# Fetching the output product's operands beside the last head pair, routing tables by one-hot products, and fillings copied by ScalarE

## The reference, cut to what matters

```python
def hybrid_layer(x, ...):
    proj = x @ w_in                                   # 2816 columns
    pool_out = multiscale_pool(proj[..., :256], pool_w, pool_scale)
    rwkv_out = rwkv7_mix(proj[..., 256:], ...)        # 12 heads of 64
    mixed = concatenate([pool_out, rwkv_out]) @ w_out
    h = layer_norm(ALPHA * x + mixed, ln1_g, ln1_b)
    ffn = hierarchical_moe(h, ...)
    return layer_norm(ALPHA * h + ffn, ln2_g, ln2_b)

def hierarchical_moe(h, ...):                         # top group, two experts of 32
    dest = pstart[e_sorted] + (arange(m) - start[e_sorted])
    row_tok = zeros(m_pad, int32).at[dest].set(tok_sorted)   # table: row -> token
    block_expert = minimum(searchsorted(pend, block_start, side='right'), 31)
    for each block of 128 rows:                       # 47 blocks here
        xb = h[row_tok[block]]
        ys = (silu(xb @ exp_gate[e]) * (xb @ exp_up[e])) @ exp_down[e]
```

## Time and profile before

| what | us |
|---|---|
| median of 3 runs (4409.91 to 4419.05) | 4418.75 |
| the profiled execution's own time | 4415.78 |
| its span, first to last instruction | 4414.0 |
| TensorE busy | 3847.3 (87%) |
| VectorE, ScalarE, GpSimd busy | 1659.9, 1159.3, 560.0 |
| mean granted TensorE clock | 0.948 |

### The profile page before, as it was taken

The page is one execution under the profiler, slowest core; times in us unless marked ns, Lnnn a source line. Parts: engine busy times, 40 slices in busy tenths (PEclk is TensorE's granted clock), DMA queues, the critical chain, the costliest instruction groups (busy, mean ns, idle before and its releaser), DMA issues.

```text
span 4414.0 us, 56437 instructions
## 1 busy us (share of the span) xinstructions
PE 3847.3 (87%) x24468; PEld 2362.1 (54%) x24468; DVE 1659.9 (38%) x2549; ACT 1159.3 (26%) x1953; POOL 560.0 (13%) x523
## 2 busy tenths in 40 slices
PE   7899999879699999378898988988688899989989
PEld 3466656544277776034455555555344466546654
DVE  2455455522211111742344444444121544354431
ACT  1222222210011111022233333333111344434440
POOL 0121212101200000320111110100000200020001
PEclk8999999979899999688999999999798999999999
DMA  3000000022599997750000000000310000000001
GB/s 99 15 16 20 16 16 21 1 107 96 167 387 364 367 368 283 261 164 10 15 15 15 15 15 15 5 6 20 108 39 20 10 1 1 12 1 1 1 29 67
DMA packets 110174, 352.07 MB, mean 80 GB/s; under 512 B 14151, under 2 KB 40118, under 8 KB 91750
## 3 DMA queue, kind: packets, MB, share of 16 engines
q1 hardware_dynamic: 86038, 290.10, 18.1%
q0 software_dynamic: 9584, 33.04, 2.2%
q10 hardware_dynamic: 14304, 25.32, 1.7%
HBM read 301.68 MB, written 46.74 MB: 79 GB/s over the span
## 4 chain that ended last, share of the span: by engine, by line
PE 71%; DVE 12%; issue 6%; DMA 4%; POOL 3%; ACT 3%; SPq 1%; ACTq 0%; POOLq 0%; DVEq 0%
PE ps L2222 9%; PE ps L1509 7%; PE ps L1871 7%; PE ps L383 7%; PE ps L2839 6%; PE ps L2240 4%; PE ps L1898 4%; PE ps L1526 4%; PE ps L1139 2%; PE ps L2547 2%; DVE sb L1845 2%; PE ps L2780 2%; PE ps L2801 1%; PE ps L450 1%; PE ps L461 1%
## 5 line engine op out<-in xcount | busy, mean ns | idle before, releaser
L2222 PE MATMUL ps<-sb 128*128 128x512 f32 x960 | 473.9, 611 | 57.7 <-DVE sb L2353 22.1
L1871 PEld LDWEIGHTS ps<-sb 128*128 128x128 f32 x2624 | 298.0, 144 | 340.3 <-ACT sb L1879 131.4
L1871 PE MATMUL ps<-sb 128*128 128x128 f32 x2624 | 427.5, 287 | 48.0 <-ACT sb L1855 18.5
L1879 ACT ACTIVATE sb<-ps 128x512 f32<-128x512 f32 x400 | 238.8, 597 | 791.8 <-PE ps L1871 791.8
L1855 ACT ACTIVATE sb<-ps,sb 128x1280 f32<-128x1280 f32 (+1 forms) x288 | 352.0, 1229 | 143.3 <-DVE sb L1848 140.5
L383 PE MATMUL ps<-sb 128*128 128x512 f32 x704 | 357.0, 622 | 3.4 <-DMA sb<-in_w_in 3.4
L1509 PE MATMUL ps<-sb 128*128 128x256 f32 x1504 | 342.2, 381 | 2.1 <-DMA sb<-in_exp_down 1.3
L2839 PE MATMUL ps<-sb 96*128 96x512 f32 (+1 forms) x768 | 337.5, 533 | 0.0
L1886 DVE COPY sb<-ps 128x512 f32<-128x512 f32 x256 | 176.9, 691 | 415.4 <-PE ps L1871 415.2
L1898 PEld LDWEIGHTS ps<-sb 128*64 128x64 f32 x5248 | 290.2, 139 | 72.1 <-ACT sb L1879 37.0
L1898 PE MATMUL ps<-sb 128*64 128x128 f32 x5248 | 325.9, 279 | 2.9 <-DVE sb L1886 1.6
(11 more groups left out here) (343 smaller groups left out, 4812.0 us busy)
## 6 DMA issues: line engine op xcount, KB each, us to landing
sb<-in_exp_gate SPq DMA_DIRECT2D x47, 1024.0 KB
sb<-in_exp_up SPq DMA_DIRECT2D x47, 1024.0 KB
sb<-in_exp_down SPq DMA_DIRECT2D x47, 1024.0 KB
sb<-in_l_w_mod ACTq DMA_DIRECT2D x12, 2048.0 KB
d_ys<-sb SPq DMA_DIRECT2D x47, 512.0 KB, 14.1
sb<-d_x SPq DMA_DIRECT2D x40, 512.0 KB
sb<-in_l_w_in SPq DMA_DIRECT2D x3, 4096.0 KB, 13.2
sb<-in_w_in SPq DMA_DIRECT2D x22, 512.0 KB, 4.2
```

The costliest lines, as they stand in the source:

```text
L1871: ins = k.pe.e.transpose(k.bank(6)[:, 128 * j:128 * j + 128], self.Pb[g % 2][:, 1280 * b + 128 * c:1280 * b + 128 * c + 128], k.f(C_ID, 128))
L1879: k.act.e.activation(self.PT[:, xs[0]:xs[-1] + 1, :], k.bank(6)[:, 0:128 * len(xs)].rearrange("p (j t) -> p j t", j=len(xs)), ACT.Copy).th ...
L2222: ins = pe.e.matmul(k.bank(5), lhs[:, kk, :], w[:, kk, 512 * half:512 * half + 512], start=kk == 0, stop=kk == 7)
```

## The change

1. **Output product.** The barrier after `mixers` goes. A new object `Ahead` fetches `w_out` into the place of the (now used up) x and projection weights, six mixed rows, the router rows, then the seventh mixed row, two x tiles and the norm rows, from two steps (`ahead`, 0) and (`ahead`, 1) on SyncE, placed behind the last filling and between the merges of the last pair. The eighth mixed row isn't fetched: the product reads `fsq` in SBUF and waits for it only at k = 7. The order inside a tile becomes half 0, half 1 up to k = 3, transposes of the tile before, half 1 from k = 4, router of the tile before.
2. **Routing.** The 16 scatters, the zeroing, the read-back and the transpose go. VectorE makes two one-hot tables (`block`, times the token number, and `place`), and TensorE multiplies them, 16 matmuls of 128x128 by 128x47. SyncE's weight fetches now wait for `beI` alone. Slices: 0 before the counts, 1 and 2 after them, 3 after the row tables; 4 and 5 are fetched at block 43 of the loop and multiplied behind it, the remaining adds move to tiles 1 to 7 (two in tile 7).
3. **Fillings.** `b'z` goes to banks 6 and 7 in matmuls of its own, and ScalarE copies it into `zb` without a mask; VectorE keeps the wide masked copy. GpSimd's level masks wait for ScalarE's copies. `k_next[:2]` moves from ahead of the filling to the steps beside the merges.
4. **Pooling.** `pool_mm` 0 stands behind project(3), and `pool_mm` 1 behind the k projection of pair 0.

```diff
-    for j in range(2):
-        order += project(2 + j) + [("pool_z", j), ("pool_sum", j), ("pool_mm", j)]
+    order += project(2) + [("pool_z", 0), ("pool_sum", 0)] + project(3) + [("pool_mm", 0), ("pool_z", 1), ("pool_sum", 1)]
-    order += k_next + weave(r_next, decay(0) + [("kk", 0), ("kk_sq", 0)])
+    order += k_next + [("pool_mm", 1)] + weave(r_next, decay(0) + [("kk", 0), ("kk_sq", 0)])
     for f in range(6):
-        order += [("zr", f, 1)]
+        order += [("zr", f, 1)] + fill(f) + [("rk", f)]
-            order += k_next[:2] + fill(f) + [("rk", f)]
-            beside = weave(beside + decay(f + 1), k_next[2:] + r_next[:8]) + ...
+            beside = weave(beside + decay(f + 1), k_next + r_next[:8]) + ...
         else:
-            order += fill(f) + [("rk", f)] + weave(merges(0), beside) + weave(merges(1), scan(f, 0)) + ... + finish(f)
+            order += [("ahead", 0)] + weave(merges(0), beside) + [("ahead", 1)] + weave(merges(1), scan(f, 0)) + ... + finish(f)[:-1]
...
+            pe.wait_ge(*t["bT"])
+            for h in range(2):
+                pe.wait_ge(*free[6 + h])
+                ins = pe.e.matmul(k.bank(6 + h)[:, 0:128], bT[halves[h], cs], zr[halves[h], c, 0, :], start=True, stop=True)
+            ins.then_inc(*product.up())
+            t["zbmm"] = product.at
...
+            act.wait_ge(*t["zbmm"])
+            act.e.activation(zb[c // 4][up, j2, :], v[up, :, 0:128], ACT.Copy)
+            act.e.activation(zb[c // 4][low, j2, 0:64], v[low, :, 64:128], ACT.Copy).then_inc(*evac_a.up())
+            free[6] = free[7] = t["zb", c // 4] = evac_a.at
...
-            dve.e.tensor_tensor(zb[g][up, j2, :], v[up, :, 0:128], bc(k.sb[up, C_MA:C_MA + 128], 1, 2), ALU.mult)
-            dve.e.tensor_tensor(zb[g][low, j2, 0:64], v[low, :, 64:128], bc(k.sb[low, C_MA + 64:C_MA + 128], 1, 2), ALU.mult)
...
+        elif kind == "ahead" and x[0] == 0:
+            sp.wait_ge(*t["proj", 1])
+            ahead.fetch_weights()
+            for n in ("lora", "km", "bT0", "kT", "bT"):
+                sp.wait_ge(*t[n])
+            for half in range(2):
+                sp.wait_ge(*t["zr", half])
+            sp.wait_ge(*t["mix"])
+            ahead.fetch_mix(range(6))
+            ahead.fetch_rows()
+        elif kind == "ahead":
+            for n in ("rk", "tailturn", "bv", "mix"):
+                sp.wait_ge(*t[n])
+            ahead.fetch_mix((6,))
+            for n in range(2):
+                ahead.fetch_x(n)
+            ahead.fetch_norm()
...
+            order += [("product", n, 0, 0), ("product", n, 0, 1), ("sum", n, 0), ("product", n, 1, 0)]
         if n:
-            order += [("turn", n - 1), ("route", n - 1)]
+            order.append(("turn", n - 1))
+        if n < NT:
+            order += [("product", n, 1, 1), ("sum", n, 1), ("norm", n), ("scale", n)]
+        if n:
+            order.append(("route", n - 1))
...
+            for kk in range(4 * part, 4 * part + 4):
+                pe.wait_ge(*wo_in[kk].at)
+                if kk == 7:
+                    pe.wait_ge(*ahead.last)
...
+        dve.e.tensor_scalar(pc, d16, 1.0 / 128, None, ALU.mult)
+        dve.e.tensor_tensor(past, bc(pc, 2, 48), bc(k.f(C_BI, 48), 1, 16), ALU.is_ge)
+        dve.e.tensor_reduce(n_past, past, AX, ALU.add)
+        dve.e.scalar_tensor_tensor(out=pc, in0=n_past, scalar=-128.0, in1=d16, op0=ALU.mult, op1=ALU.add)
+        dve.e.tensor_tensor(block, past[:, :, 0:47], past[:, :, 1:48], ALU.subtract)
+        for j in range(2):
+            dve.e.tensor_tensor(v, v, bc(tokv, 2, 47), ALU.mult)
+        dve.e.tensor_tensor(place, bc(pc, 2, 128), bc(k.f(C_IP, 128), 1, 16), ALU.is_equal)
...
         for c in range(16):
-            pool.e.indirect_dma_start(out=dr["rows"], ...)
+            ins = pe.e.matmul(k.bank(2)[:, 0:NBLK], place[:, c, :], block[:, c, :], start=c == 0, stop=c == 15)
...
-    for i in range(2):
-        mod.pe_product(i, 3 + i)
-        mod.act_fetch(i + 2)
+    mod.pe_product(0, 3)
+    mod.act_fetch(2)
     counted = pe_counts(t_oh)
+    mod.pe_product(1, 4)
+    mod.act_fetch(3)
+    mod.pe_product(2, 5)
     t_be, t_dst = dve_places(counted)
-    t_sc = pool_scatter(t_dst)
+    t_turn = pe_rows(dve_row_hots())
+    dve.e.tensor_copy(rowI[:, 0:NBLK], k.bank(2)[:, 0:NBLK])
+    mod.pe_product(3, 6)
+    t_wt = dve_weights(t_gexp, t_eexp)
+    for i in range(4):
+        mod.dve_add(i, 3 + i)
+        mod.act_store(i)
+        mod.act_fetch_bias(i + 2)
...
-    sp.wait_ge(*t_sc)
...
-        mixers(k, a, dr, const_in.at)
-        k.stage_end()
-        mod = out_and_norm(k, a, dr, const_in.at)
+        ahead = mixers(k, a, dr, const_in.at)
+        mod = out_and_norm(k, a, dr, const_in.at, ahead)
```

More of the change, by code:

```diff
@@ L28 @@
 C_LV = 1024
+C_IP = C_LV + 448
 C_SC = C_LV + 7 * 128
@@ L356, in mixers @@
         else:
-            order += fill(f) + [("rk", f)] + weave(merges(0), beside) + weave(merges(1), scan(f, 0)) + scan(f, 1) + [("scan_end",)] + finish(f)
+            order += [("ahead", 0)] + weave(merges(0), beside) + [("ahead", 1)] + weave(merges(1), scan(f, 0)) + scan(f, 1) + [("scan_end",)] + finish(f)[:-1]
     def pe_program(kind, *x):
@@ L1119, in out_and_norm @@
-    t["rows"] = row_in.at
     order = []
@@ L1171, in act_program @@
         elif kind == "modulation":
+            for tok in (ahead.scanned, ahead.last):
+                act.wait_ge(*tok)
             made.append(Modulation(k, a, dr))
     def dve_program(kind, *x):
-        if kind == "product":
-            n = x[0]
+        if kind == "sum":
+            n, half = x
             s = n % 2
+            dve.wait_ge(*ahead.scanned)
             dve.wait_ge(*t["x", n])
@@ L1180, in dve_program @@
             dve.wait_ge(*t["hturn", s])
-            for half in range(2):
-                hs = slice(512 * half, 512 * half + 512)
-                dve.wait_ge(*t["mm", half])
-                dve.e.scalar_tensor_tensor(out=hr[s][:, hs], in0=xr[s][:, hs], scalar=ALPHA, in1=k.bank(2 * s + half), op0=ALU.mult, op1=ALU.add).then_inc(*evac_v.up())
-                free[2 * s + half] = t["sum"] = evac_v.at
+            hs = slice(512 * half, 512 * half + 512)
+            dve.wait_ge(*t["mm", half])
+            dve.e.scalar_tensor_tensor(out=hr[s][:, hs], in0=xr[s][:, hs], scalar=ALPHA, in1=k.bank(2 * s + half), op0=ALU.mult, op1=ALU.add).then_inc(*evac_v.up())
+            free[2 * s + half] = t["sum"] = evac_v.at
         elif kind == "norm":
@@ L1208, in sp_program @@
     def sp_program(kind, *x):
-        if kind == "product" and x[0] + 2 < NT:
+        if kind == "sum" and x[1] == 1 and x[0] + 2 < NT:
             sp.wait_ge(*t["sum"])
-            load_x(x[0] + 2)
+            ahead.fetch_x(x[0] + 2)
         elif kind == "scale":
@@ L1286, in experts @@
     cnt, nb, pend, pst = new(32), new(32), new(32), new(32)
-    gt, des, le, be, rw = new(32, 8), new(8, 2), new(48, 32), new(48), new(128)
+    gt, des, le, be, n_past = new(32, 8), new(8, 2), new(48, 32), new(48), new(16)
+    pc, later = new(16), take(4096)
+    past = k.f(later, 768).rearrange("p (c b) -> p c b", c=16)
+    block = k.f(later + 768, 752).rearrange("p (c b) -> p c b", c=16)
+    place = k.f(later + 2048, 2048).rearrange("p (c b) -> p c b", c=16)
     def dve_top_group():
@@ L1490, in experts @@
             order.append(("down", b - 1))
+        if b == NBLK - 4:
+            order.append(("mod", b))
     def pe_program(kind, b):
@@ L1532, in act_program @@
         s = b % 2
-        if kind == "turn":
+        if kind == "mod":
+            for i in (4, 5):
+                mod.act_fetch(i)
+        elif kind == "turn":
             act.wait_ge(*t["turn", 1])
@@ L3160, in program @@
     dr = {}
-    for name, shape in (("mix", [8, P, S]), ("h", [S, D]), ("rows", [NBLK * P, 1]), ("ys", [NBLK * P, D]), ("x1", [S, D]), ("x2", [S, D]),
+    for name, shape in (("mix", [8, P, S]), ("h", [S, D]), ("ys", [NBLK * P, D]), ("x1", [S, D]), ("x2", [S, D]),
                         ("ctx1", [256, D]), ("mod", [2, 2, 3 * D])):
```

200 lines of the change are left out of this document (102 added, 98 removed).

## The result

| | before | after |
|---|---|---|
| median of all runs, us | 4418.9 (4409.91 to 4419.9, 4 runs) | 4296.69 (4294.42 to 4301.94, 4 runs) |
| profiled execution's own time | 4415.78 | 4297.71 |
| its span | 4414.0 | 4296.0 |
| TensorE busy | 3847.3 | 3827.3 |
| mean granted clock | 0.948 | 0.959 |

The ratio is 0.973, 95% interval 0.9713 to 0.9746. Forecast were 4327 us and a range of 4302 to 4357: the direction holds, the gain is 122 us where 92 were worked out. TensorE's busy time fell by 20 us; the other 98 of the span are idle time that is gone.

What follows compares the result with a forecast made beforehand. TensorE, busy 87% of the span, was taken as the bound. 37.7 + 23 + 16 + 16 - 1 = 92 us off the profiled 4415.8 gave 4324, plus 3 for the median: 4327 us, range 4302 to 4357.

Steps and rivals of the forecast that it cites:

- Seam, 37.7 us: Before and in the output product: barrier, late fetches and router waits go, 37.7 us gained, bounds 28 and 39.
- the rival in which they don't: Output product's fetches from SyncE come late and the change turns slower: 4425 us or more, chance 0.02.
- Pooling, +16: Early stretch: 17.8 us of waits for pooling sums and cold restarts go, less new delays; gain 16, bounds 9 and 21.
- The late step it named: Pooling: the second pooled row's store stands ahead of the first decay, whose ScalarE step waits for it; 4 us.
- Fillings, +16: Fillings of the pairs: 2.5 to 3 us a pair, last pair 4.5, 16 us with a margin for the new hand-shake.
- the charge for the moved projection steps: Fillings: 1.7 us of projection move from where TensorE waited 0.5 to 1 us into a stretch busy 35.95 of 39.
- The rule on weight loads: Fillings: a load costs its columns; twelve unhidden make 1.28 us a chunk, not 1.15, and the gain 6 us less.
- Head, +23: Start of the experts' stage: second gate at t0 + 63.7 instead of 86.7, gain 23 us, bounds 16 and 32.
- the first rival: Experts' head: the modulation slice lands early, so the head gains 31 us instead of 23, 4319 us; chance 0.13.
- Tail, -1: Behind the experts' loop: the adds move one tile on, costing 0 to 4 us, taken as -1.
- the 2 us at which the prediction was to be wrong in an unnamed way: Sign: gate distance in the loop or the stages behind 1856 us changing by over 2 us means an unnamed error.
- the sum of 92: Whole kernel: seam 37.7, head 23, pooling 16, fillings 16 and tail -1 make 92 us gained.

Runs made afterwards that it cites:

- p_copies: Kernel after with VectorE's masked b-z copies from banks 0 to 3 back, the two projection steps left in their new place; median 4331.55 us.
- p_slice_late: Kernel after with the fetch of the fourth modulation slice held on ScalarE until the one-hot tables are made; median 4320.74 us.
- q_mask_late: Kernel after with one wait added per filling: GpSimd's first mask of a group also waits for VectorE's masked copy of its last chunk; median 4307.86 us.
- q_weights_late: Kernel after with SyncE's expert weight fetches held until the row table is there; median 4307.76 us.
- p_tiles: Kernel after with a tile's turn and router product behind the whole next product again, operands still fetched ahead; median 4311.98 us.
- b_store_wait: Kernel after, but VectorE's scan instead of ScalarE's first sigmoids waits for the second pooled row's store; median 4295.5 us.

## Why the prediction was wrong

Point by point:

- **Seam, 37.7 us**: right in mechanism, 3 us too small and over its own upper bound of 39. From the last gate product to the product's end it is 170.4 us before and 129.6 after, 40.7 gained. Undone in two pieces it is 33.1 + 7.1 = 40.2, where 32.1 and 5.6 were said. SyncE's fetches all came in time; the rival in which they don't falls.
- **Pooling, +16**: right, 15.1. The late step it named, ScalarE behind the store of the second row, cost what was said: 4 forecast; taken away, the product came 2.8 us and the first filling 4.4 us sooner.
- **Fillings, +16**: mis-sized; they gave 22.1 us up to the last pair's exponentials and 3.8 in the last filling (43.7 to 39.9 us from the exponentials to the second merge), 26 in all. The step that failed is the charge for the moved projection steps, "1.7 us of projection move out of a spot where TensorE waited for ScalarE anyway (0.5 to 1 us of it) into a stretch where it was busy 35.95 of 39 us", from which 2.5 to 3 us a pair came. As worded the charge is 0.5 to 1 us, which would leave 3.6 to 4.1 a pair; the 2.5 to 3 charge 1.6 to 2.1. The other two terms held: 2.9 us for the shorter filling (3 said) and 1.7 for the second group (1.6 said). In the pairs 1 to 4, from the middle of the last projection to the second group's merge, it is 20.2 us before (289.7, after four of the eight projection passes of 287.73 to 291.62, to 309.86) and 15.0 after (404.97 to 419.98); the rest of the pair's distance is 116.7 and 116.2. So the two steps left the front with all their 1.9 us, paid 1.3 there for the new start, and cost nothing among the merges. Such a pair gives 5.7 us, 5.3 in the mean of the four (two took 132.0 instead of 131.2). In the first pair, where no finish of an earlier pair is woven in, the charge was real: from the second group's merge to the next exponentials it is 88.9 us before and 90.4 after, and the whole pair gave 0.8. p_copies adds what I had not seen: the steps were cover for VectorE, and the two edits are worth 5.3 to 5.7 together while moving the steps alone is worth nothing.
- **The rule on weight loads**. The Trainium skill ("TensorE: Matmul & The Clock Gate", "LDWEIGHTS (loading the stationary operand)") makes a load cost by its columns, and twelve unhidden loads of 107 ns would be 1.28 us a chunk, an estimate from that page. The twelve passes of a chunk took 1.08 us (407.95 to 409.03), so the loads were hidden in part at least. The 1.26 us of the bare chunks has ScalarE's 0.16 us and small gaps in it.
- **Head, +23**: mis-sized, 32.1, and the first rival (0.13) is what happened. The chain was right: VectorE copies the counts at t0 + 10.5 (10.3 said), the block table is there at t0 + 18.0 (17.8), the destinations at t0 + 21.2 (21.1), the one-hot tables at t0 + 27.6 (28). The one-hot product took 7.07 us, where 4 were said from a row at full clock; it ran at 0.50 after 2.9 us of idle, and so the rows came at t0 + 44.5 (42.3). In p_slice_late the same product took 5.8 us at 0.62. The step that failed is "Its fetch and the experts' weights start together at t0 + 17", with "26, so it is there at t0 + 44". The slice was issued about 1.5 us ahead and was there 15.8 us later, by t0 + 34. The reading of the queues itself, equal counts of packets once both flow, was right, and p_slice_late shows it charging even more than 26 us. The Trainium skill ("DMA: Bandwidth & Descriptors", "Queues, rings and completion order") has an engine take turns between the queues packet by packet. From 1078 us on the counts agree (162 and 185); in the four microseconds before, 19 and 675, they do not.
- **Tail, -1**: not told from nothing. The loop kept its length. The stages behind it came 2.5 us shorter, over the 2 us at which the prediction was to be wrong in an unnamed way, but kernels with the same tail differ there by more (last section).
- **The time before**: the profiled execution lay 3 us under its median and the one after 1 over it, so the medians differ by 4 more than the spans do.
- **Slips without effect**: the eight operations of the one-hot tables add to 5120 elements, not 5112, and 12 us for them is the row at half its rate, not at a third.

Against the sum of 92 the profiled executions give 118: fillings 10 more, head 9, seam 3, the stages behind the loop 3.5, the unsteady piece of the last pair 2 (0.91 of the clock where it had been 0.89), pooling 1 less. Both large errors were made on the same side: each had a price for a collision (steps into a busy stretch, a slice among the weights) that did not take place, but for the first pair. The median, 4296.7, lies where the prediction had put all its favourable bounds taken at once (4296).

## What to carry to other kernels

Before charging for a step that is moved into a busy stretch, subtract the idle that its new neighbours have there pair by pair, and ask what the step had covered in its old place. When two queues meet, look at the order of issue to the microsecond: here the slice that went 0.8 us ahead landed in 17 us and the one 2.5 us behind in 33. A part of 5 us is read between two marks close around it, not from the whole time, and the granted clock between the marks is read with it: one piece of 90 us differed by 6 from kernel to kernel with the same instructions.

## What the runs showed of the hardware that was not expected

**The second queue starts late.** With the slice ahead, SyncE's first weight packets moved about 4 us after their issue (19 packets up to 1078 us in the kernel after, issue at 1073.4); with nothing ahead of it, in p_slice_late, they moved about 1 us after (issue at 1070.7). It holds the other way round too: in p_slice_late the slice, issued into the weights at about 1079.5, moved its first packets behind 1083. Why the first queue keeps the engines was not found.

**GpSimd beside VectorE.** The 128x512 mask took 1.27 us alone or beside VectorE's operations that read PSUM. Started inside VectorE's 128x1024 operation on SBUF it took 2.18 us in all four such cases of q_mask_late and 2.24 or 2.25 in all five of the kernel before. Started ahead of that operation it kept its 1.27 us, and VectorE's operation took 1.57 instead of 1.28. Either way it is the later of the two that is longer.

**The clock in one piece.** The piece of the last pair named ahead of the experiments took 86.4 us at 0.96 of the clock, 91 at 0.91 and 92.5 at 0.89, with some 1237 recorded passes each time.

**The clock behind the loop.** The stages behind the experts' loop are the same instructions in all kernels here but for the first 100 us, and took 2649.0 (p_slice_late) to 2663.9 us (q_weights_late), 2656.0 in the kernel after and 2663.3 in p_tiles. Two stretches of TensorE, 1400 to 1600 us behind the last down product, in the kernel after, p_tiles and p_slice_late (length, busy, granted clock, DMA share, GB/s):

```profile
3040.00:3140.00 100.00, 87.98 (x271) 0.93 0.15 53
3140.00:3240.00 100.00, 91.02 (x277) 0.98 0.02 6
```

```profile
3045.10:3145.10 100.00, 87.26 (x269) 0.93 0.15 53
3145.10:3245.10 100.00, 91.04 (x268) 0.93 0.02 6
```

```profile
3063.80:3163.80 100.00, 89.14 (x286) 0.98 0.14 50
3163.80:3263.80 100.00, 87.21 (x267) 1.00 0.05 14
```

The granted clock differs there by 0.05 to 0.07 with the same work; what makes it differ is open. The profiled p_tiles is 12.4 us longer than the kernel after, 7.1 at its place and 7.3 behind the loop. For b_store_wait, 4 us ahead by its edit, the profiled execution is 13.4 us shorter and the median 1.2: a whole time doesn't show a part of that size.
